# Rounding weight i+2 on ScalarE directly behind the unit that used weight i-1

## The reference

```
# first block, per layer
h = rms_norm(x, norm_g); p = h @ w_in            
y_a = short convolution of cc*cx, times cb*silu(cgate), @ w_out_conv
y_b = top-k sparse attention (indexer iq, ik, iw), * silu(gate), @ w_out_attn
y_c = pooled means over 2, 4, 8, 16 tokens, @ pool_w, * silu(gate), @ w_out_pool
x = x + (g0*y_a + g1*y_b + g2*y_c) @ w_o         # g = sigmoid(mgate)
# second block, per layer
three branches of one norm: attention (8 query, 2 key heads, axial rope),
a Hyena mixer (long convolutions as DFT products), gated linear attention;
merged by gates, @ an output matrix, added to x
cross attention to a memory of 256 tokens, added to x
mlp: x = x + act(norm(x) @ w1) @ w2              # 4096 wide
```

## Time and profile before

| | |
|---|---|
| median of 3 runs | 3255.43 us (3254.47 to 3259.03) |
| the profiled execution | 3252.9 us |
| its span on the core | 3250.9 us, mean granted clock 0.998 |
| TensorE busy | 3223.4 us (99%) |
| VectorE, GpSimd, ScalarE busy | 1613.1, 1570.8, 1292.0 us |
| DMA engines busy | 37% |
| HBM | 316.02 MB read, 25.30 MB written |

### The profile page before, as it was taken

One profiled execution on the slowest core, in us unless ns is written; L12 is line 12 of the kernel. 1 busy time (PEld: TensorE's weight loads), 2 busy tenths in 40 slices (PEclk: granted clock), 3 DMA queues, 4 the chain that ended last, 5 costly groups with the idle time before them and its releaser, 6 DMA issues.

```text
span 3250.9 us, 40100 instructions
## 1 busy us (share of the span) xinstructions
PE 3223.4 (99%) x15156; PEld 2547.6 (78%) x15156; DVE 1613.1 (50%) x2736; ACT 1292.0 (40%) x1984; POOL 1570.8 (48%) x1224
## 2 busy tenths in 40 slices
PE   9999999999999999999999999999999999999999
PEld 7788778787877767767788888887676788888887
DVE  4566433546543678864555321227887455442020
ACT  4343643334464322454446322232235544642231
POOL 4554334545434563334463565646333446446473
PEclk9999999999999999999999999999999999999999
DMA  4323224323223523452353433334236235334332
GB/s 158 98 84 97 75 88 147 120 94 92 81 84 91 184 98 101 142 145 81 112 182 98 130 118 97 102 122 139 91 119 166 77 112 187 118 117 123 97 91 97
DMA packets 145976, 370.16 MB, mean 114 GB/s; under 512 B 18670, under 2 KB 35630, under 8 KB 145784
## 3 DMA queue, kind: packets, MB, share of 16 engines
q1 hardware_dynamic: 145784, 367.60, 37.0%
HBM read 316.02 MB, written 25.30 MB: 105 GB/s over the span
## 4 chain that ended last, share of the span: by engine, by line
PE 93%; DVE 4%; ACT 2%; issue 1%; POOL 1%; DMA 0%; SPq 0%; DVEq 0%; ACTq 0%
PE B L942 27%; PE B L944 27%; PE B L943 27%; PE B L1007 1%; PE B L1111 1%; PE B L1134 1%; PE B L1167 1%; PE B L1209 1%; PE B L1217 1%; PE B L1198 1%; POOL WSP L1732 1%; PE B L1082 1%; PE B L1073 1%; PE B L1148 1%; PE B L1203 0%
## 5 line engine op out<-in xcount | busy, mean ns | idle before, releaser
L1732 POOL TENSOR_TENSOR WSP<-WRAW,WSP 128x512 fp32r<-128x512 f32 x1036 | 1359.0, 1333 | 1469.9 <-ACT WSP L1350 1469.4
L942 PE MATMUL B<-H,WSP 128*128 128x512 f32 x2496 | 993.0, 398 | 7.7 <-POOL WSP L1732 7.7
L944 PE MATMUL B<-H,WSP 128*128 128x512 f32 x2496 | 972.6, 390 | 0.0
L943 PE MATMUL B<-H,WSP 128*128 128x512 f32 x2496 | 971.9, 389 | 0.0
L1350 ACT ACTIVATE WSP<-WRAW 128x1024 fp32r<-128x1024 f32 (+1 forms) x567 | 555.8, 984 | 669.3 <-PE B L944 528.7
L942 PEld LDWEIGHTS B<-H,WSP 128*128 128x128 f32 x2496 | 468.8, 188 | 127.6 <-issue 25.3
L943 PEld LDWEIGHTS B<-H,WSP 128*128 128x128 f32 x2496 | 469.0, 188 | 100.9 <-issue 6.9
L944 PEld LDWEIGHTS B<-H,WSP 128*128 128x128 f32 x2496 | 468.5, 188 | 99.0
L1815 DVE TENSOR_TENSOR B<-B,RN 128x512 f32<-128x512 f32 x194 | 134.8, 697 | 392.1 <-PE B L944 375.8
L942 PE MATMUL B<-YM,WSP 128*128 128x512 f32 x512 | 199.5, 390 | 0.0
L944 PE MATMUL B<-YM,WSP 128*128 128x512 f32 x512 | 199.2, 389 | 0.0
(11 more groups left out here) (451 smaller groups left out, 4806.8 us busy)
## 6 DMA issues: line engine op xcount, KB each, us to landing
WRAW<-in_wb SPq DMA_DIRECT2D x318, 512.0 KB, 3.7
WRAW<-in_wa SPq DMA_DIRECT2D x153, 512.0 KB, 3.7
PTB<-BLK SPq DMA_DIRECT2D x128, 128.0 KB, 2.7
WRAW<-in_wa SPq DMA_DIRECT2D x50, 256.0 KB, 2.6
WRAW<-in_wb SPq DMA_DIRECT2D x48, 256.0 KB, 2.6
parked<-HYT SPq DMA_DIRECT2D x24, 256.0 KB, 2.1
QA<-RXA SPq DMA_DIRECT2D x64, 64.0 KB, 2.0
xs<-PA SPq DMA_DIRECT2D x16, 256.0 KB, 4.4
```

Of the source, the lines that this page charges most:

```text
L942: e.matmul(o, L[0], R[0], start=first, stop=False)
L943: e.matmul(o, L[0], R[1], start=False, stop=False)
L944: return e.matmul(o, L[1], R[0], start=False, stop=last)
L1732: x = e.tensor_tensor(WSP[:, i % NSP, 1, c:c + CUT], WRAW[:, i % NRAW, c:c + CUT], WSP[:, i % NSP, 0, c:c + CUT].bitcast(fp32), ALU.subtract)
```

## The change

Only ScalarE's loop is edited. The rounding that stood at the head of the unit of weight i (for weight i+2) now stands at the start of the unit that follows the unit of weight i-1 in the plan, whatever that is. Where two units with weights follow each other directly this is the same place; where weightless units lie between them, the rounding now comes ahead of ScalarE's part of these. Units of kind `woa` keep the old place, and so does the second weight of a unit with two.

```diff
             own = [0]
-            for u in plan:
+            begun = None
+            for behind, u in zip([None] + plan, plan):
                 k, a = u.kind, u.a
                 if own[-1] != act_done.n:
                     w.value(act_done.sem, own[-1])
                     own.append(act_done.n)
+                if behind and behind.w and behind.kind != "woa":
+                    next_halves(behind.w0 + len(behind.w) + NSP - 1)
                 for g in range(len(u.w)):
-                    if u.w0 + g:
+                    if g or begun and begun.kind == "woa":
                         next_halves(u.w0 + g + NSP - 1)
+                begun = u if u.w else begun
```

## The result

The change makes the kernel slower: 3331.5 us (median of 4 runs, 3327.5 to 3343.8) against 3255.0 (3253.2 to 3259.0). The ratio is 1.024, with a 95% interval of 1.0209 to 1.0270. Slower was forecast, but by 24 us and not by 77: 3279 us, range 3262 to 3300. The sign was right, and so were most of the places; the size was a third of what was measured.

The account below looks back on a forecast made before the run. TensorE, busy 3223.4 of 3250.9 us, was taken to bound the kernel. Costs of 34.5 us less gains of 8.9 made 25.6, so 3281 by the median, less 2 for loads catching up: 3279 us, range 3262 to 3300.

Parts of the forecast that it names:

- key norms: Second block's attention, both layers: late raw weight's rounding delays the square root, TensorE 4.3 us late each; cost 8.6 us.
- the third Hyena turn: Evacuation of the third token turn stands behind a late raw weight's rounding; 2.7 us late, twice, cost 5.4 us.
- linear attention: Roundings go ahead of the state product's evacuation in both layers (2.1 us) and the gate exponentials (0.9); cost 3.0 us.
- the output products: First block's second layer 5 us, second block 2.4 in each layer; first block's first layer nothing.
- the ring: Output products: raw load, rounding, two ScalarE norm instructions, residual reload, next raw load; turn 7.0 us against TensorE's 5.45.
- rival (d): Ring terms doubled plus 2.4 us of clock: 3292 us; over 3300 with late cross-attention loads; chance above 3292: 0.13.
- the clock: Two new 4.3 us waits might each bring a slow stretch, 2.4 us more, near 3281; left out of the sum.
- attention of the first block: Roundings waiting for raw weights stand ahead of scaling the probabilities TensorE transposes; places in both layers, cost 7.7 us.
- the block at 898 us: A long block in the first block's attention, said to have most of its cover; cost 0.3 us.
- The terms of 3.3 and 1.1: Gains: 1.65 us wait behind exponentials and a square root, with its twin, 3.3; output weight behind linear attention's scan, 1.1.
- the longest wait: TensorE's 5.46 us wait for a low half whose rounding stands behind the gated-linear-attention norm; net gain 4.5 us.
- Rival (a): Raw loads come earlier with the earlier roundings, so only gains are left: 3246 us; chance 0.08.

Follow-up runs that it names:

- experiments 7: Against before: only roundings of weights 230 and 413 moved, ahead of the key norms, raw weight requested ahead of the eight key exchange transfers; 3252.5 us, ratio 0.9993.
- 8: Every raw weight requested one unit earlier in SyncE's queue: changed kernel 3266.8 us; before 3250.3; before with only four roundings moved (weights 243, 259, 274, 426) 3241.7.
- experiment 1: Changed kernel, but roundings with a norm unit between old and new place (the output-product stages) keep the old place; 3293.9 us, ratio 1.0108.
- experiment 3: Changed kernel with SyncE's reloads of residual chunks 4 to 7 issued behind the next unit's raw load; 3297.5 us, ratio 1.0120.
- experiment 6: Against before: only roundings of weights 230 and 413 moved, and TensorE issues four unread constant products ahead of the query norm's sums; 3267.3 us, ratio 1.0030.

## Why the forecast was right in sign and wrong in size

**What held.** That TensorE has 27.5 us to win and no bound on what it can lose. That a moved rounding blocks ScalarE's queue where its raw weight lands late, because SyncE's order did not move: experiments 7 and 8 show it. The named places are in the trace. Their idle time was 7.1 for 8.6 forecast (key norms), 4.8 for 5.4 (the third Hyena turn; 1.3 more at a second rounding that was not priced), 4.1 for 3.0 (linear attention).

**The step that failed first: the output products.** They were put at 9.8 us and cost 36. Two errors are in the term. The turn was put at 7.0 us and is 7.9, as VectorE's low half (1.2 us), for which the reload waits, was left out of the ring. Four such turns in a stage, which the forecast had right, are then about 9.8 us too slow and not 6.4, and the five or so in hand, which were to protect the first block's first layer, do not cover it. And three of the six stages were put at nothing: "The same ring in the first layer has over 5 us in hand and costs nothing", and the cross attention's two stand nowhere in the sum, only in rival (d). By the stretches of experiment 1 these three cost 6.3, 6.1 and 6.0 us, 18 in all; the three that were priced at 5.0, 2.4 and 2.4 cost 7.4, 8.0 and 3.1. That all six are the ring through SyncE's reload is shown by experiment 3.

**The second: the clock.** The sum left it out "because those waits are broken by small matmuls". They were not protected: behind the key norms' waits of 3.4 us the granted clock was at 0.58 and 0.56, and lower clock was added behind other new waits from 1.7 us on. It makes 26 of the 33 us by which TensorE was busy longer; at the key norms the slower work costs about as much as the idle time itself in the traces. The Trainium skill (TensorE: Matmul & The Clock Gate, "Part 1: The HAM clock gate") says that an array left idle falls back to half its clock. These rows agree as to the level; the 1.00 behind a wait of 2.67 us shows that the length of the one wait does not tell whether it falls. The forecast set its price beside the sum, for two places, where it belonged in it for all. The 1.2 us taken for a wait would still have been too little at the key norms, which show about 3 us each.

**The third: attention of the first block.** Idle 12.8 us for 7.7. The 3.1 at 938 us was measured as 2.6, the 1.7 of its twin as 1.8. But the block at 898 us, put at 0.3, cost 2.7 at two transposes, of which 1.0 was given back, and three places were not priced at all: 1.2, 0.6 and 1.2 us, at 178, 326 and 365 us of the changed kernel.

**The gains.** 8.9 forecast; 6.9 by the delays in the changed kernel. The terms of 3.3 and 1.1 came as 3.8 and 1.2; the 4.5 of the longest wait as 1.9, since another result of the same busy ScalarE is late next.

Rival (a), that loads come earlier by themselves, fell as argued. The load that was to decide it, at 1319.55 in before, goes out at 1358.84 in the changed kernel, later by the 39.3 us by which TensorE is late there: SyncE's queue had to be changed for it. Rival (d), rings and clock at their worst, was the nearest with 3292 us and still too low, as it doubled the ring term where it had to be taken nearly four times; its last clause, the cross attention, was worth 12 us.

What stays open: the 21 us of the first block's attention were not taken apart rounding by rounding, and it is not clear why the clock fell in layer 1 of experiment 6 in spite of 3.6 us of filling, nor why it stayed up behind some waits and not behind others. What the key norms cost by themselves is 6.5 to 13 us by the time.

## What to carry to other kernels

Moving a producer's step ahead of other work in an in-order queue moves its wait as well: look first at when its input arrives, and move the request for the input before the step. Where the step closes a ring with a transfer, compare the ring's turn with the consumer's pace; if it is longer, count its turns: the loss is turns times the difference, less the time in hand. Walk the ring through every engine that stands in it, as one step left out is paid at each turn. Price the new waits of a TensorE that is busy 99% with the slower work behind them as well; here it cost two thirds as much again as the waits.

## What the runs showed of the hardware

The granted clock fell behind shorter waits than I had expected, but not behind all. A wait of 1.65 us left it at 1.00. In the changed kernel it was 0.57 behind a wait of 2.10 us and 0.58 behind 3.39, and full speed came back within 4 us in the first case and after 8 us in the second. Behind the 5.46 us of before it had been 0.60, no lower than behind 2.10. Three waits of 1.74 to 1.84 us (at 396, 412 and 979 us) were followed by 0.50 to 0.58 as well. Of the twelve waits between 2.0 and 2.7 us eight were followed by the lower level and four, of 2.17, 2.22, 2.30 and 2.67 us, by 1.00. So in this trace one wait's length does not tell whether the clock falls; the slower work is priced as a sum over many waits.
